# Router before the norm and expert 0 on a free side path, in a two-layer mixture-of-experts trunk

## The reference

```python
x = layer_norm(ALPHA * x + m, ln_mix_g[i], ln_mix_b[i])      # m: the mixer's output
logits = x @ router_w                                        # fp32, 16 experts in 4 groups
scores = sigmoid(logits); biased = scores + router_bias
group = argmax(sum of the top 2 of biased in each group)
expert_idx = top 2 of biased in that group
w = scores at expert_idx, divided by their sum
y = sum over e of gates[:, e] * ((silu(x @ w_gate[e]) * (x @ w_up[e])) @ w_down[e])
x = layer_norm(ALPHA * x + y, ln_ffn_g[i], ln_ffn_b[i])
```

## Time and profile before

| | us |
|---|---|
| median of 3 runs | 1205.08 (1204.64 to 1205.65) |
| profiled execution | 1205.72 |
| its span, first to last instruction | 1204.1 |
| TensorE busy | 1076.1 (89%) |
| VectorE busy | 856.1 (71%) |
| ScalarE busy | 673.3 (56%) |

### The profile page before, as it was taken

The page is one execution under the profiler, slowest core; times in us unless marked ns, Lnnn a source line. Parts: engine busy times, 40 slices in busy tenths (PEclk is TensorE's granted clock), DMA queues, the critical chain, the costliest instruction groups (busy, mean ns, idle before and its releaser), DMA issues.

```text
span 1204.1 us, 15212 instructions
## 1 busy us (share of the span) xinstructions
PE 1076.1 (89%) x5264; PEld 854.4 (71%) x5264; DVE 856.1 (71%) x1005; ACT 673.3 (56%) x771; POOL 118.5 (10%) x158
## 2 busy tenths in 40 slices
PE   6999998399999999938999999999389999999960
PEld 5888886277777777726887888887267777777740
DVE  4454556789999988966615455436779999989938
ACT  4322324378888888842417333223468888888841
POOL 1000000101111121310000000000101111112212
PEclk9999998599999999977999999999689999999985
DMA  8224422589999999954214222421499999999933
GB/s 316 89 85 194 140 106 105 186 306 373 379 378 394 378 371 391 396 202 191 110 48 174 72 76 100 176 87 38 164 326 329 392 378 378 385 384 370 391 107 148
DMA packets 50061, 289.31 MB, mean 240 GB/s; under 512 B 9168, under 2 KB 9296, under 8 KB 20304
## 3 DMA queue, kind: packets, MB, share of 16 engines
q1 hardware_dynamic: 36816, 255.87, 55.8%
q0 software_dynamic: 8336, 17.32, 4.3%
q10 hardware_dynamic: 4848, 15.31, 3.4%
HBM read 277.98 MB, written 23.07 MB: 250 GB/s over the span
## 4 chain that ended last, share of the span: by engine, by line
PE 65%; issue 21%; DVE 5%; POOL 4%; DMA 4%; ACT 1%; SPq 0%; POOLq 0%; ACTq 0%; DVEq 0%
PE ps L438 20%; PE ps L440 20%; PE ps L439 20%; POOL y_rows L502 2%; DMA xg<-x_rows,idx_col 1%; PE ps L1592 1%; POOL xg L495 1%; PE ps L1780 1%; PE ps L1655 1%; DMA Y<-y_rows 1%; PE ps L1584 1%; DVE hot L467 1%; DVE stats L1202 1%; DVE X L1210 1%; DVE X L1402 1%
## 5 line engine op out<-in xcount | busy, mean ns | idle before, releaser
L434 DVE TENSOR_TENSOR lo<-raw,hi 128x1024 fp32r<-128x1024 f32 x336 | 397.8, 1221 | 98.5 <-ACT hi L427 96.4
L427 ACT ACTIVATE hi<-raw 128x1024 fp32r<-128x1024 f32 x336 | 347.5, 1058 | 117.5 <-PE ps L440 101.3
L438 PE MATMUL ps<-hi,xgT_hi 128*112 128x512 f32 x512 | 204.7, 400 | 5.6 <-DVE xgT_lo L1329 5.6
L440 PE MATMUL ps<-hi,xgT_lo 128*112 128x512 f32 x512 | 202.6, 396 | 0.0
L439 PE MATMUL ps<-lo,xgT_hi 128*112 128x512 f32 x512 | 201.6, 394 | 0.0
L434 DVE TENSOR_TENSOR lo<-raw_more,hi 128x1024 fp32r<-128x1024 f32 x128 | 155.9, 1223 | 20.8 <-ACT hi L427 13.4
L427 ACT ACTIVATE hi<-raw_more 128x1024 fp32r<-128x1024 f32 x128 | 135.0, 1059 | 43.6 <-PE ps L440 32.2
L438 PE MATMUL ps<-xT_hi,hi 128*128 128x512 f32 x320 | 127.3, 398 | 12.7 <-DVE lo L434 11.1
L439 PE MATMUL ps<-xT_lo,hi 128*128 128x512 f32 x320 | 125.5, 392 | 0.0
L440 PE MATMUL ps<-xT_hi,lo 128*128 128x512 f32 x320 | 125.5, 392 | 0.0
L438 PEld LDWEIGHTS ps<-hi,xgT_hi 128*112 128x112 f32 x512 | 90.3, 176 | 32.9 <-DVE xgT_lo L1329 6.7
(11 more groups left out here) (175 smaller groups left out, 1402.2 us busy)
## 6 DMA issues: line engine op xcount, KB each, us to landing
raw<-in_w_moe SPq DMA_DIRECT2D x128, 1024.0 KB, 11.3
raw_more<-in_w_moe SPq DMA_DIRECT2D x64, 1024.0 KB, 11.4
raw<-in_w_dense SPq DMA_DIRECT2D x40, 1024.0 KB, 4.8
Y<-y_rows SPq DMA_DIRECT2D x16, 512.0 KB, 7.2
x_rows<-X ACTq DMA_DIRECT2D x8, 512.0 KB, 2.6
xT_raw<-in_x_t SPq DMA_DIRECT2D x4, 512.0 KB, 8.8
X<-in_x SPq DMA_DIRECT2D x1, 2048.0 KB, 9.3
mix_par<-in_ln_par ACTq DMA_DIRECT2D x4, 512.0 KB, 8.7
```

The source lines that it names most:

```text
L427: nc.scalar.activation(hi[:, s, :], flat(raw_units(n)), ACT.Copy).then_inc(hi_ready, 1)
L434: eng.tensor_tensor(lo[:, s, :], flat(raw_units(n)), hi[:, s, :], ALU.subtract).then_inc(lo_ready, 1)
L438: nc.tensor.matmul(out_, a_hi, b_hi, start=first, stop=False)
L440: return nc.tensor.matmul(out_, a_lo, b_hi, start=False, stop=last)
```

## The change

The router works on the residual before its norm. With r the un-normalised row, the logits are (r @ W2) * rstd + c2, where W2 is the router's weights times the gain, less its column mean, and c2 the offsets times the weights, summed. W2 and c2 are made for each layer on the chip: gains and offsets come as `rgb` (16 x 128), `router_turn` turns them, `router_prod` multiplies, `router_sums` sums over the partitions by a product with ones, `router_weights` puts W2 and c2 together. Logits come out by token, so that `by_token` is gone.

Each tile is turned before it is normalised: the norm waits for the turn. `place_slots` (positions and one-hots) is cut off from `route` and runs after the next tile's moments. Row numbers are made in two groups: experts 0 to 2 (`NA` = 3) first, the other 13 during gate/up of expert 0.

Expert 0 has no gather: its turned rows `x0` are the sum over tiles of X[t] times a one-hot `hot0` (112 columns) in fp32 (`first_rows`). Its weight units are not split but used as they came, in fp32 (`gate_up_first`, `down_first`), and their buffers are free when TensorE has used them. The scaling by ALPHA moves from ScalarE into the addition of the first half of the experts' output.

```diff
+WHOLE = {n for l in (0, 1) for n in [gu0(l, 0) + k for k in range(GU)] + [dn0(l, 0) + k for k in range(DN)]}
...
                 if RAW_BEFORE[n] is not None:
-                    wait_lo(sp, RAW_BEFORE[n] + 1, step, i)
+                    m = RAW_BEFORE[n]
+                    if m in WHOLE:
+                        sp.wait_ge(unit_used, m + 2)
+                    else:
+                        wait_lo(sp, m + 1, step, i)
...
+                for t in range(NT):
+                    preload(ACT.Sqrt)
+                    root(8 * layer + t, t)
+                    router_in(layer, t)
                     preload(ACT.Sigmoid)
+                    scores(layer, t)
+                    act.wait_ge(normed, 8 * layer + t + 1)
+                    act.dma_start(x_rows[t * P:(t + 1) * P, :], X[:, t, :]).then_inc(xrow_out[t], 16)
+                for k in range(4):
+                    split_hi(act, gu0(layer, 1) + k)
...
             params(1, 0, mix_par[1])
+            act.dma_start(rgb[1][:, :], ln_par[1, 0, :, :].rearrange("g (k p) -> (g k) p", p=P)).then_inc(rgb_in[1], 16)
...
+                for t in range(NT):
+                    mixed(layer, t)
+                    if t:
+                        place_slots(layer, t - 1)
+                    dve.wait_ge(tr_ready, TR_MIX[layer] + 2 * t + 2)
+                    norm(8 * layer + t, t, mix_par[layer], 1 + 2 * layer)
+                    route(layer, t)
+                place_slots(layer, NT - 1)
+                route_ids(layer, True)
...
+                dve.wait_ge(xgT_ready, m0 + 1)
+                nc.vector.tensor_copy(x0[:, 4:8, 0:T], slots(ps[:, 6:7, :])).then_inc(xgT_lo_ready, 1)
+                for k in range(4):
+                    own_lo(gu0(layer, 1) + k)
+                for t in range(NT):
+                    slots_hot(dve, hot[layer][t], posm, t, slice(NA, E)).then_inc(hot_ready, 1)
+                route_ids(layer, False)
+                route_most(layer)
+                x_lo(1)
+                hidden(0)
+                for k in range(4, GU):
+                    own_lo(gu0(layer, 1) + k)
+                route_gates(layer)
...
-                mix(layer, 1, {2: (T(0),), 3: (L(0),)})
-                mix(layer, 2, {0: (B(0),), 2: (T(1),), 3: (C(0),)})
-                mix(layer, 3, {0: (I(0), L(1)), 1: (B(1),), 2: (T(2), C(1)), 3: (L(2),)})
-                for f in (B(2), I(1), T(3), L(3), C(2), B(3), I(2), C(3), I(3)):
-                    f()
...
+                mix(layer, 1, {0: (T_(0),), 1: (L(0),)})
+                mix(layer, 2, {0: (C(0), T_(1)), 1: (L(1),)})
+                mix(layer, 3, {0: (C(1), T_(2)), 1: (L(2),)})
+                positions(layer, 2)
+                T_(3)()
+                first_rows(layer, 0)
+                logits(layer, 3)
+                first_rows(layer, 1)
+                first_ids(layer, 0)
+                first_ids(layer, 1)
+                first_rows(layer, 2)
+                first_ids(layer, 2)
+                positions(layer, 3)
+                first_rows(layer, 3)
+                first_ids(layer, 3)
...
+                    for k in range(GU):
+                        n = gu0(layer, 0) + k
+                        wait_raw(pe, n)
+                        for h in range(2):
+                            ins = nc.tensor.matmul(ps[0:T, h, :], x0[:, k, 0:T], flat(raw_units(n))[:, h * F:(h + 1) * F],
+                                                   start=(k == 0), stop=(k == GU - 1))
+                        ins.then_inc(unit_used, 1)
+                        if k == 4:
+                            counts(layer)
+                            other_ids(layer)
+                        if k == GU - 2:
+                            turn_x(1)
...
+                gate_up_first()
                 turn_h(0)
+                gate_up(1)
+                gates_to_slots(layer)
+                turn_x(2)
+                down_first()
+                turn_h(1)
                 turn(1)
...
             for m in range(8):
                 n, s = SO0 + m, slot_of(SO0 + m)
                 wait_lo(pe, n)
+                if m == 4:
+                    pe.wait_ge(sg_taken, NC)
+                    router_turn(1)
+                if m == 6:
+                    pe.wait_ge(ones_ready, 1)
+                    router_sums(1, ones_g)
...
+            def router_turn(layer):
+
+                pe.wait_ge(rgb_in[layer], 16)
+                nc.tensor.transpose(ps[:, 6, 0:2 * KD], rgb[layer][:, :], ident[0:2 * KD, 0:2 * KD]).then_inc(rgb_tr, 1)
```

More of the change, by code:

```diff
@@ L99, in last_users @@
         out.append(last.get(slot(n)))
-        last[slot(n)] = n
-    return out
-BEFORE, RAW_BEFORE = last_users(slot_of), last_users(raw_slot)
-LO = [n + 1 for n in range(UNITS)]
+        if n not in skip:
+            last[slot(n)] = n
+    return out
+BEFORE, RAW_BEFORE = last_users(slot_of, WHOLE), last_users(raw_slot)
+LO = [sum(m not in WHOLE for m in range(n + 1)) for n in range(UNITS)]
 INDEX = list(range(UNITS))
@@ L463, in gated, with slots_hot, rows_by_slot @@
             return xT_hi[:, j - NC // 2, :], xT_lo[:, j - NC // 2, :]
[L465 to L470, removed]
+        def slots_hot(eng, out_, pos, t, es=slice(0, E)):
+            n = es.stop - es.start
+            return eng.tensor_tensor(out_[:, es, :], iota_s[:, None, :].to_broadcast([P, n, P]),
+                                     pos[:, t, es, None].to_broadcast([P, n, P]), ALU.is_equal)
+        def rows_by_slot(chain, layer, es=slice(0, E)):
             by = scr[layer]["by_slot"]
[L473 to L476, removed]
+            chain.step(nc.vector.scalar_tensor_tensor(out=by[:, es, 0], in0=by[:, es, 2], scalar=no_row[:, 1:2],
+                                                      in1=by[:, es, 0], op0=ALU.mult, op1=ALU.add))
+            return nc.vector.scalar_tensor_tensor(out=idx[:, es], in0=by[:, es, 0], scalar=no_row[:, 0:1],
+                                                  in1=by[:, es, 1], op0=ALU.add, op1=ALU.add)
         def gates_of_slots(chain, layer):
@@ L824, in experts @@
                     pool.wait_ge(xrow_out[t], 16 * (layer + 1))
[L825 to L826 removed]
+                pool.wait_ge(idx_ready, 2 * layer + 1)
+                for e in range(1, NA):
                     fetch(layer, e)
+                pool.wait_ge(idx_ready, 2 * layer + 2)
                 def turn(e, i=0):
@@ L900, in _ @@
             spatial_weights(ws_sum)
-            with act.Fori(0, 2) as i:
-                conv_tile(2, i, (12, 13, 14))
-                conv_tile(3, i, (15, 16, 17))
+            for c in range(2, 6):
+                conv_tile(c, 0, (3 * c + 6, 3 * c + 7, 3 * c + 8))
             conv_tile(6, 0, (24, 25, 26, 27, 28))
@@ L928, in scores, with norm_and_route @@
             def scores(layer, t):
-                if t < NT - 1:
-                    preload(ACT.Sigmoid)
[L931 to L961, removed]
-                ahead(2, 2)
-                router_in(layer, 3)
-                preload(ACT.Sigmoid)
-                scores(layer, 3)
-                ahead(4, 1)
-                residual(layer, 2)
-                ahead(5, 3)
+                act.wait_ge(lgt_ready, NT * layer + t + 1)
+                nc.scalar.activation(score[:, t, :], scr[layer]["lgt"][:, :], ACT.Sigmoid).then_inc(sig_ready, 1)
+            def norm_and_route(layer):
+                for t in range(NT):
+                    preload(ACT.Sqrt)
+                    root(8 * layer + t, t)
+                    router_in(layer, t)
+                    preload(ACT.Sigmoid)
+                    scores(layer, t)
[3 more added lines that the diff above has]
+                    split_hi(act, gu0(layer, 1) + k)
             def experts(layer):
@@ L1396, in combine @@
                     dve.wait_ge(first_in[t], 16 * (layer + 1))
-                    chain.post(nc.vector.tensor_tensor(X[:, t, :], X[:, t, :], Y[layer][0][:, t, :], ALU.add))
+                    chain.post(nc.vector.scalar_tensor_tensor(out=X[:, t, :], in0=X[:, t, :], scalar=ALPHA,
+                                                              in1=Y[layer][0][:, t, :], op0=ALU.mult, op1=ALU.add))
                 def first(t):
@@ L1649, in turn_x @@
                 def turn_x(c, i=0):
-                    pe.wait_ge(xg_in[c % 2], plus(16 * ((c + m0) // 2 + 1), i, 16))
+                    pe.wait_ge(xg_in[c % 2], plus(16 * gathers(layer, c), i, 16))
                     if c + m0:
```

261 lines of the change are left out of this document (170 added, 91 removed).

## The result

The changed kernel took 1196.99 us (median of 4 runs, 1196.13 to 1197.85), the kernel before 1205.37 in the same rounds: a ratio of 0.9934, 95% interval 0.9922 to 0.9945, so 8.4 us faster. The forecast was 1194, with 1180 to 1201 as its range. The profiled execution took 1197.66 us, its span is 1196.0, 8.1 less than before.

The account below looks back on a forecast made before the run. TensorE was taken to set the time, losing it at layer boundaries. Terms -13.3 - 12.8 - 4.2 + 1.0 + 1.6 + 16.5 = -11.2 us from the 1205.08 median gave 1194 us, range 1180 to 1201.

Parts of the forecast that it names:

- The way from E to expert 0: From E, the end of a layer's last mixing product, to gate/up of expert 0: E+14.1 to 15.6 instead of 34.
- the wait at the ids: In expert 0's gate/up, TensorE arrives at E+22.9 or 25.2 and waits for the other experts' ids, summed at 27.0.
- gate/up of expert 2 comes at about E+57: First point where both kernels do the same: E+56.1, or 57.6 if colder, middle 56.8, against 70.1 and 69.6.
- the colder case: TensorE at half clock before expert 0: first_rows(3) takes 3.1 us, not 1.54; gate/up of expert 2 at E+57.6.
- The new wait in layer 1: TensorE at router_turn waits 14.0 us for gains and offsets queued behind three transfers; with 2.4 for half clock, +16.5.
- rival (a): Layer 1's small router transfer overtakes: wait 4.4 us, no clock loss, about 1182 (1177 if never waited for); chance 0.14.
- The mixing stretch: From tile 0's products to E: 39.0 us instead of 41.1, so 2.1 us less in each layer.
- rival (b): Weight stream limits the first experts: late units cost 2 to 4 us in each layer, 1198 to 1202; chance 0.17.
- The clock at the ids: A second fall of TensorE's clock during the ids wait, in one of the layers: +1 us.
- The boundary as a whole: From E to gate/up of expert 2: 13.3 us less in layer 0 and 12.8 less in layer 1.
- Router parameters on TensorE: Column sums over the router weights and a small turn: 0.8 us of TensorE in each layer, +1.6 together.
- The end of layer 0: Stage from the turn for expert 15 to layer 1's first pass over xT_hi, put at +14.0 us.

Follow-up runs that it names:

- the run with a gather: Changed kernel with first_rows left out, so GpSimd gathers expert 0's rows and they are turned as before: 1212.1 us.
- The early transfer: Changed kernel with layer 1's router gains and offsets issued after the split of gated row 12, nothing ahead on ScalarE's queue: 1181.2 us.
- the one first in the queue: Changed kernel with layer 1's router parameter transfer ahead of the 2 MB reload and two broadcasts, at the same moment: 1180.7 us.
- The narrow passes: Changed kernel plus 16 unread fp32 passes per tile, 16 columns of weights and 16 streamed, ahead of the logits: 1204.0 us.
- the runs with down split: Down of expert 0 split, three passes: on the changed kernel 1192.6 us; with early transfer and both changes of order too, 1170.0 us.

## Why the prediction was right, and where its sum was off

**The way from E to expert 0** was right: E+14.3, put at 14.1 to 15.6. So was the wait at the ids and that gate/up of expert 2 comes at about E+57: 56.7 and 56.1, put at 56.8. Reading the chain of each engine in its program order gave this to 1 us. TensorE didn't cool before expert 0, so the colder case that I allowed for didn't come. The gather's removal is 9.8 of the 26.8 us gained here (15.1 by the medians of the run with a gather); the other 17.0 come with the router ahead of the norm and what goes with it, not taken apart.

**The new wait in layer 1** was right in place, length and cause: 13.7 us against 14.0, landing after the three others. The early transfer brought 15.8 back, against 16.5 put at it; the one first in the queue landed in 1.7 us. That it overtakes, rival (a), is thereby refuted for this place in the queue.

**The mixing stretch** is the step that failed, by the size of one term. I put the new logits at 1.0 us a tile, "between them", in bounds of 0.4 and 1.85. They take 1.69, and 33.1 + 2.7 + 3 x 1.69 + 0.2 gives the 41.1 that was measured. So the stretch lost nothing where I had 2.1 us less per layer: 4.2 of the sum. The bound that I took for the upper one, passes with 16 columns of weights and 128 streamed, was nearly the price; the lower one, from bf16 loads, was not to be had. The narrow passes show that it is the wide load in fp32 that costs, 0.106 us against 0.03. The Trainium skill (page "TensorE: Matmul & The Clock Gate", section "Weight-path perf modes — Fast Weight Load (FWL) and DoubleRow") gives no fast load of weights to fp32. I had this beside the bounds and gave it no weight; it agrees with these numbers.

**The weight stream** was rival (b), with 2 to 4 us a layer and a chance of 0.17. It was there with its mechanism, at 1.1 and 1.6 us in the profiled execution (0 to 3.0 a layer over eight traces), and not in the sum. That it hangs on the late release of expert 0's down units is shown by the runs with down split, which have none of it. Why it stays away in some executions without the split isn't shown.

**The clock at the ids**: I put 1 us, in one layer; it fell in both, 1.7 us each. The boundary as a whole came out as put all the same, so other small terms in it were too dear by as much.

Router parameters on TensorE seem to cost 0.4 us in layer 0, where I had 0.8, but executions differ by more there.

**The end of layer 0** was 1.9 us better than put, and the two traces say where. The last of the experts' outputs was added 44.4 us after the turn for expert 15 and not 45.4, since its reload landed sooner: 1.0 us. Behind the wait for the norm TensorE ran at half clock for 3.6 us (536.7 to 540.3) and not 5.7 (549.7 to 555.4): 1.0 us. It looks like luck of the execution and not like a gain: from the turn for expert 15 to tile 0 added in layer 1, the changed kernel has 323.4 us, and the five others with the same wait for the parameters have 324.2 to 326.4, against 325.7 by the forecast's terms. In the traces the sum misses by 3 us; without this it would miss by 5. Of the changed kernel's other executions there is no trace.

## What to carry to other kernels

Before a transfer is put behind others on a queue, ask who will wait for it: 8 KB behind 3 MB landed 12.1 us after their issue, and their place alone was worth 13.6 us in the trace. A wait that is taken away uncovers the next one in program order on another engine, so change the orders together and measure them together. Buffers that are held longer at the start of a stream can cost later and elsewhere, in experts that the edit doesn't touch, and not in every execution alike; here 0 to 3.0 us a layer.

## What the runs showed of the hardware

An fp32 pass with 128 columns of weights and 16 streamed took 0.106 us, with 16 columns of weights 0.03, and the bf16 id sums with 128 columns 0.025. So in fp32 the wide load was not hidden behind the narrow product.

TensorE's clock fell from 2.4 to 1.2 GHz while the profile has it busy without a gap: behind 3.4 us of logits passes, three times in one mixing stretch (window clock 0.90, busy 51.0 of 51.0). Behind 1.7 us of them it stayed at full. A busy share of 100% was thus no warrant for the clock. What in these passes brings it down, no run here separates.
